# A hybrid decoder step: the sample tokens of the delta-rule group as one masked chunk on TensorE

## The reference, cut to what matters

```python
def step(S, inp):
    rt, wt, kt, vt, kkt, at = inp
    sa = jnp.einsum('nhij,nhj->nhi', S, -kkt)
    S = (S * wt[:, :, None, :] + sa[..., None] * (kkt * at)[:, :, None, :]
         + vt[..., None] * kt[:, :, None, :])
    return S, jnp.einsum('nhij,nhj->nhi', S, rt)
S, y = lax.scan(step, s0.astype(F32), ...)      # over the tokens of a sequence
y = (y - mean(y)) * rsqrt(var(y) + eps)         # per head, then gain, offset, bonus
```

## Time and profile before

| | |
|---|---|
| median of 3 runs | 3367.37 us (3344.56 to 3388.64) |
| the profiled execution's own time | 3341.69 us |
| its span, first to last instruction | 3339.8 us |
| mean granted clock of TensorE | 0.928 of full speed |
| PE busy | 2920.4 us, 87% |
| DVE busy | 1480.7 us, 44% |
| ACT busy | 915.8 us, 27% |
| POOL busy | 83.5 us, 2% |
| the stage `rwkv`, layer 1 | about 1245 to 1452 us of the span |
| the stage `rwkv`, layer 2 | about 2857 to 3066 us of the span |

### The profile page before, as it was taken

The page is one execution under the profiler, slowest core; times in us unless marked ns, Lnnn a source line. Parts: engine busy times, 40 slices in busy tenths (PEclk is TensorE's granted clock), DMA queues, the critical chain, the costliest instruction groups (busy, mean ns, idle before and its releaser), DMA issues. The chain is left out here.

```text
span 3339.8 us, 62897 instructions
## 1 busy us (share of the span) xinstructions
PE 2920.4 (87%) x26036; PEld 2706.7 (81%) x26036; DVE 1480.7 (44%) x2589; ACT 915.8 (27%) x1733; POOL 83.5 (2%) x132
## 2 busy tenths in 40 slices
PE   3999999999887986879889999999988779686995
PEld 2998989997775876769879898899877578675994
DVE  0532253225734567852243225322574347586322
ACT  2322242123221342222142224321322115322222
POOL 0010000000000000000001000000000000000000
PEclk8998999999998998979999999999999869896997
DMA  3322334432233221033223233443323313202431
GB/s 139 91 72 68 84 93 134 136 98 71 51 95 81 64 84 46 3 133 112 85 73 83 62 83 98 112 140 107 85 51 89 93 44 81 72 3 83 127 111 61
DMA packets 413106, 283.74 MB, mean 85 GB/s; under 512 B 44204, under 2 KB 385900, under 8 KB 408334
## 3 DMA queue, kind: packets, MB, share of 16 engines
q1 hardware_dynamic: 412238, 275.19, 29.3%
q10 hardware_dynamic: 576, 4.46, 0.3%
HBM read 243.39 MB, written 36.18 MB: 84 GB/s over the span
## 5 line engine op out<-in xcount | busy, mean ns | idle before, releaser
L359 PE MATMUL acc<-h_hi,in_w_hi 128*128 128x272 f32 x3968 | 904.9, 310 | 40.3 <-SPq L534 18.9
L359 PE MATMUL acc<-h_lo,in_w_hi 128*128 128x272 f32 x3968 | 838.5, 293 | 0.0
L359 PE MATMUL acc<-h_hi,in_w_lo 128*128 128x272 f32 x3968 | 837.5, 293 | 0.0
L359 PEld LDWEIGHTS acc<-h_hi,in_w_hi 128*128 128x128 f32 x3968 | 644.6, 195 | 102.8 <-issue 46.2
L359 PEld LDWEIGHTS acc<-h_lo,in_w_hi 128*128 128x128 f32 x3968 | 642.8, 194 | 0.0
L359 PEld LDWEIGHTS acc<-h_hi,in_w_lo 128*128 128x128 f32 x3968 | 639.4, 194 | 0.0
L386 DVE TENSOR_TENSOR in_w_lo<-in_w_raw,in_w_hi 128x512 fp32r<-128x512 f32 x496 | 349.2, 710 | 482.2 <-ACT in_w_hi L382 479.6
L382 ACT CAST in_w_hi<-in_w_raw 128x512 fp32r<-128x512 f32 x496 | 303.1, 617 | 455.5 <-PE acc L359 373.3
L359 PE MATMUL out_acc<-mix_hi,out_w_hi 128*128 128x272 f32 x1024 | 214.6, 291 | 22.8 <-DVE mix_lo L722 22.7
L359 PE MATMUL out_acc<-mix_hi,out_w_lo 128*128 128x272 f32 x1024 | 213.9, 291 | 0.0
L359 PE MATMUL out_acc<-mix_lo,out_w_hi 128*128 128x272 f32 x1024 | 213.2, 290 | 0.0
(11 more groups left out here) (393 smaller groups left out, 3612.2 us busy)
## 6 DMA issues: line engine op xcount, KB each, us to landing
in_w_raw<-in_w_in SPq DMA_DIRECT2D x488, 256.0 KB, 2.9
region<-in_cache_sb_kv SPq DMA_DIRECT2D x128, 256.0 KB, 3.1
out_w_raw<-in_w_out SPq DMA_DIRECT2D x128, 256.0 KB, 2.7
regions<-in_cache_dsa SPq DMA_DIRECT2D x64, 160.0 KB, 2.1
region<-x_spill SPq DMA_DIRECT2D x8, 1088.0 KB, 9.0
x_spill<-region SPq DMA_DIRECT2D x32, 272.0 KB, 2.1
mix_spill<-mix SPq DMA_DIRECT2D x6, 1088.0 KB, 5.5
mix_back<-mix_spill SPq DMA_DIRECT2D x6, 1088.0 KB, 7.4
```

The source lines that it names most:

```text
L359: last = pe.matmul(self.acc[:, i % 2, c, 0:HALF_N], w[:, u % RING, t, :], part[:, f, HALF_N * c:HALF_N * c + HALF_N], start=first and w is ...
```

## The change

The sample tokens are computed as one chunk of 32 tokens with masks that keep each sequence of 4 to itself (constants `s_before`, `s_upto`, `s_after`, `s_seq`), by the same algebra as the prompt's chunks, in a class `SampleRule`. Its 19 steps are set into segments of iterations 0 to 2 by the table `AT`, on PE, ACT and DVE alike, and `pool` makes three operands on POOL. PSUM grows from four to eight banks; the samples use banks 4 to 7. The state is loaded in eight transfers, one for each head, with 8x64 values for each of 64 partitions, stored in the same way, and transposed on PE both ways (steps 0, 1 and 14, 15). The trips of rows and of y through DRAM, the turning of rows, and the norm at the end are gone. `scan`, `powers` and `scale` of pairs 1 to 3, which stood ahead of iteration 0, now stand in segments 2 to 14 of iteration 0.

```diff
 class DeltaRule:
     def act(self, act):
-        act.activation(k.logw[:, :, NP:NT], k.logw[:, :, NP:NT], ACT.Exp, scale=DECAY).then_inc(kept["decayed"], 1)
-        for n in range(6):
-            act.wait_ge(made["rows"], n + 1)
-            act.copy(self.rows[n], self.bank[0:NS, n % 4, :]).then_inc(kept["rows"], 1)
-            if n < PAIRS:
-                self.powers(act, n)
+        self.powers(act, 0)
+        self.samples.powers(act)
...
+                if it == 0 and seg in (4, 9, 14):
+                    self.powers(act, seg // 5 + 1)
+                self.samples.act(act, it, seg)
...
     def dve(self, dve):
         self.scan(dve, 0)
-        self.scan(dve, 1)
-        for g in range(PAIRS):
-            self.scale(dve, g)
-            if g + 2 < PAIRS:
-                self.scan(dve, g + 2)
+        self.samples.scan(dve)
+        self.scale(dve, 0)
+        self.samples.scale(dve)
...
-                if it == 1 and seg == 2:
-                    dve.wait_ge(self.loaded, 16 * (1 + 2 * NB))
-                    self.samples.choose(dve, step)
-                if 1 <= it <= DS and seg in (3, 8, 13, 16):
-                    if seg == 3:
-                        advance = self.samples.advance(dve, step, self.summed_y, it - 1)
-                    next(advance)
+                if it == 0 and seg in (2, 7, 12):
+                    self.scan(dve, seg // 5 + 1)
+                if it == 0 and seg in (4, 9, 14):
+                    self.scale(dve, seg // 5 + 1)
+                self.samples.dve(dve, it, seg, step)
...
-        dve.wait_ge(kept["back"], 1)
-        center(PAIRS)
-        finish(PAIRS)
     def pool(self, pool):
         unit(0)
+        pool.wait_ge(kept["scaled"], PAIRS)
+        self.samples.pool(pool, self.masked)
     def sp(self, sp):
+        samples.load(sp)
         for g in range(3):
             sp.dma_start(k.mix_back[:, 4 * g:4 * g + 4, :], mix_rows(k)[g]).then_inc(self.mix_came, 16)
...
+class SampleRule:
+    AT = {(0, 0): 0, (0, 1): 1, (0, 2): 2, (0, 3): 3, (0, 5): 4, (0, 6): 5, (0, 8): 6, (0, 10): 7, (0, 11): 8,
+          (1, 2): 9, (1, 3): 10, (1, 5): 11, (1, 8): 12, (1, 11): 13, (1, 14): 14, (1, 17): 15, (2, 2): 16, (2, 4): 17, (2, 13): 18}
+    def load(self, sp):
+        for h in range(H8):
+            r, j = h % 2, h // 2
+            sp.dma_start(self.nat[C * r:C * r + C, j, :, :], self.k.state_wkv[bass.ds(self.l, 1), :, h].rearrange("a s i j -> (a i) s j")).then_inc(self.loaded, 16)
...
+    def pe(self, pe, it, seg):
+        if step in (0, 1):                     # turn the states: 32 matmuls a step
+            if step == 0:
+                pe.wait_ge(self.loaded, 16 * H8)
...
+        elif step == 9:
+            for j, r in each:
+                out = row(bank, r)[:, 7, C * j:C * j + C]
+                last = pe.matmul(out, row(self.ak, r)[:, j, :], row(self.vrow, r)[:, j, :], start=True, stop=False)
+                for s in range(NB):
+                    last = pe.matmul(out, half(self.apart, r)[:, j, NS * s:NS * s + NS], half(self.state, r)[:, j, s, :], start=False, stop=(s == NB - 1))
...
+        elif step == 11:
+            for j, r in each:
+                out = half(bank, r)[:, 5, NS * j:NS * j + NS]
+                pe.matmul(out, row(self.u, r)[:, j, :], row(self.br, r)[:, j, :], start=True, stop=False, skip_group_check=True)
+                pe.matmul(out, row(self.vrow, r)[:, j, :], row(self.ar, r)[:, j, :], start=False, stop=False, skip_group_check=True)
+                for s in range(NB):
+                    last = pe.matmul(out[:, DS * s:DS * s + DS], half(self.state, r)[:, j, s, :], half(self.w, r)[:, j, DS * s:DS * s + DS],
+                                     start=False, stop=(s == NB - 1), skip_group_check=True)
...
+        elif step in (12, 13):
+            for n in range(2):
+                j = 2 * (step - 12) + n
+                for r in range(2):
+                    out = half(bank, r)[:, (6 if step == 12 else 4) + n, :]
+                    pe.matmul(out, row(self.rows, r)[:, 1, j, :], row(self.values, r)[:, j, :, :], start=True, stop=False)
+                    last = pe.matmul(out, row(self.rows, r)[:, 0, j, :], row(self.mine, r)[:, j, :, :], start=False, stop=True)
...
+    def pool(self, pool, masked):
+        pool.memset(self.apart, 0.0).then_inc(kept["cleared"], 1)
+        for t in range(DS):
+            pool.tensor_copy(self.apart[:, :, t:NB * NS:NS + DS], self.kap[:, :, t:NS:DS]).then_inc(kept["spaced"], 1)
+        pool.wait_ge(kept["vrow"], 1)
+        pool.tensor_tensor(self.values, self.vrow[...].to_broadcast([2 * NS, 4, NB, C]), self.c("s_seq")[...], ALU.mult).then_inc(kept["values"], 1)
+        for j in range(4):
+            last = pool.tensor_tensor(self.fresh[:, j, :, :], self.state[:, j, :, :], self.ends[:, j, :].unsqueeze(2).to_broadcast([P, NB, C]), ALU.mult)
```

More of the change, by code:

```diff
@@ L135 @@
 KEPT = AT["chunk_in"][0]
+OWN_D = AT["spread"][0] - KEPT
 SPREAD = AT["spread"][0]
@@ L2174 @@
 ITER, SEGS = PAIRS + 2, 20
-MADE = "rows pair low n2 m2 vrow n4 d2 m4 brow m8 d4 krow dt d q qt q2 z key t x u y total spread final back total_s spread_s".split()
-KEPT_AS = ("rows n rest br m d1 n2 m2 vrow n4 d2 m4 brow m8 d4 krow dt d q qt q2 z ak ar t x u state y "
-           "final back scanned less up down ahead scaled ended decayed gained centered squared logged rooted mixed stepped_o").split()
+MADE = "pair low n2 m2 vrow n4 d2 m4 brow m8 d4 krow dt d q qt q2 z key t x u y total spread final".split()
+KEPT_AS = ("n rest br m d1 n2 m2 vrow n4 d2 m4 brow m8 d4 krow dt d q qt q2 z ak ar t x u state y "
+           "final scanned less up down ahead scaled ended gained centered squared logged rooted mixed normed").split()
+MADE_S = "turned pair low vrow m2 key t rows x u y grown back total spread".split()
+KEPT_S = ("turned n br m d1 vrow m2 ak ar t rows x u y mine values faded grown back spaced cleared "
+          "centered squared logged rooted normed scanned less up down ahead scaled gained aged").split()
 class DeltaRule:
@@ L2200, in __init__ @@
         self.chunk_in = free[:, 3072:3584].rearrange("p (j t) -> p j t", j=4)
-        self.sq = free[:, 3584:4096].rearrange("p (j t) -> p j t", j=4)
+        self.own = free[:, 3072:3072 + OWN_D]
+        self.sq = free[:, 3072 + OWN_D:3584 + OWN_D].rearrange("p (j t) -> p j t", j=4)
         self.ends = sb("dr_ends", [P, NC, 4])
[L2203 to L2208, removed]
         ft = k.ft
-        self.sources = (ft[:, R_SLOT:R_SLOT + 4], k.logw, ft[:, K_SLOT:K_SLOT + 4], ft[:, V_SLOT:V_SLOT + 4], k.kap, k.beta)
+        self.samples = SampleRule(k, l, take, sb, bank, free)
         self.keys, self.values, self.y = ft[:, K_SLOT:K_SLOT + 4], ft[:, V_SLOT:V_SLOT + 4], ft[:, R_SLOT:R_SLOT + 4]
@@ L2242, in pe @@
         eye = k.c("eye64")
[L2243 to L2246, removed]
-            for i in range(4):
-                last = pe.transpose(bank[0:NS, n % 4, P * i:P * i + P], t[:, i, NP:NT], k.c("ident"))
-            last.then_inc(made["rows"], 1)
-        yield 0
         def product(g, name, n, left, right):
```

339 lines of the change are left out of this document (262 added, 77 removed).

## The result

The changed kernel takes 3427.0 us (median of four runs, 3401.3 to 3450.4) against 3359.3 of the kernel before on the same chip: ratio 1.0238, 95% interval 1.0188 to 1.0288. Six more runs gave 1.0183 (1.0100 to 1.0266). Forecast were 3384 us and a range up to 3418, so it is slower than I allowed for. The medians given here are of all runs of a kernel, and a ratio leaves out the runs of either kernel that lie more than 1.5% above its fastest.

The account below looks back on a forecast made before the run. DVE looked like the bound of iterations 1 to 3, but its recurrence mostly hidden behind PE; -10.5 + 11.6 + 17.4 - 0.6 - 2.8 - 6.9 = +8.2 us a layer, +16.4 in all, gave 3384 us, range 3348 to 3418.

Parts of the forecast that it names:

- 3, *Iteration 1, +17.4 us: Iteration 1 of each layer: recurrence goes, the samples' matmuls come on PE; 56.0 us for 38.6, +17.4.
- x 4.2 to 8.4, y 4.0 to 8.0: Samples' x and y matmuls on PE in iteration 1: 58.5 to 117 ns each; taken 6.3 and 6.0 us.
- Steps 12 and 13: Samples' 16 matmuls of 512 columns on PE in iteration 1: 7.5 to 15 us, low end 7.5 taken.
- rival (c): Changes of matmul form at the samples' steps each cost 0.19 us: +10.6 us a layer, 3405 us; chance 0.09.
- Head -10.5: Stage's head: pair waits only for scan, powers and scale of pair 0, so starts 10.5 us sooner.
- Iteration 0 +11.6: Iteration 0: later pairs' scans and scales on DVE, samples' transposes and small steps on PE; 40.6 us for 29.0.
- Iteration 2: Without the recurrence t and the totals start sooner, but the samples' two totals on PE take 2.0 us: -0.6 us.
- Iteration 3: Without the recurrence t starts 1.9 us sooner and the totals 1.0, with 0.3 coming back: -2.8 us.
- Iteration 4 and the end: Iteration 4: 0, nobody waits for its recurrence; end: -6.9 us, no wait for `sample_y`, the prompt's last norm ends it.
- (b): Halves don't overlap in runs, in steps 9 to 15 of iteration 1: +23.2 us a layer, 3414 us; chance 0.12.
- (a): Matmuls overlap and fill gaps, long runs at the low end: -3.9 us a layer, 3360 us; chance 0.22.
- (d): Gain is what DVE's share promised, iterations 1 to 3 fall to PE's work: -18.5 us a layer, 3330; chance 0.05.

Follow-up runs that it names:

- e1: The changed kernel with the halves r alternating from matmul to matmul in the samples' x and y (steps 9 and 11): 3373.8 us, ratio 1.0037.
- b1: The kernel before, without the recurrence's arithmetic on VectorE (trips to DRAM, waits and stores stay): 3325.9 us, ratio 0.9924.

## Why the prediction was wrong

The step that failed is 3, *Iteration 1, +17.4 us*, and in it two terms: "x 4.2 to 8.4, y 4.0 to 8.0 ... I take the middle for the long runs". The rest of the step held. Without the samples I had iteration 1 at 27.1 + 4.8 = 31.9 us; the kernel without the recurrence has 32.6. Steps 12 and 13 are 7.3 us (taken 7.5), the transposes 3.7 (3.8), and u is 1.0 at the low clock and 0.6 in e1 (0.5).

x and y failed by order and by clock. The order: at the full clock a group of x takes 1.23 us and a group of y 1.37, that is 9.8 and 11.0 us, above even my high ends of 8.4 and 8.0, since a matmul in a run of one half takes 128 ns (two records of 64) and two interleaved halves do two in the same time. My bound of 117 ns was twice the right row; I took the middle because runs of two go at full speed, and from two in a row nothing follows for nine. The rule that I quoted from the Trainium skill ("TensorE: Matmul & The Clock Gate", part 3, "The mechanism": a weight load overlaps matmuls in flight only in another row group) fits the trace of after, 64 ns a record against 32; but the halves here differ in the partitions that they write as well, and no run tells the two apart, nor why runs of two go free. The changes of form cost little, as I said against rival (c): two records with another form ahead of 16 take 0.23 us, 0.1 more than two in the row, for two changes.

The clock: no term and no rival had a fall of it, only the last sentence ("a PE clock below 1.00 in iteration 1"). It is 8 of the 28.8 us, and some 3.3 more in the prompt's products behind both runs (e1 gains 20.3 from key to key, 17.0 of it in x and y).

With this one term mended, the sum comes out right, in part by luck. e1 has x and y at 5.0 and 6.8 us, close to the 6.3 and 6.0 in my sum, and its stages are 7.4 and 7.6 us longer than before; the forecast was 8.2 a layer. It measures 1.0037, and the forecast was 1.005. Up to the last key product e1 is 19.6 us longer than before, where the sum has 15.1, and from there on 12.1 shorter, where it has 6.9: two errors of some 5 us that cancel.

The other steps. Head -10.5: it is -10.6 (8.5 us for 19.1). Iteration 0 +11.6: +13.9, with brow at 17.4 us from pair, dt at 24.7 and q2 at 34.3 (walked: 17.9, 25.0, 34.5); the missing 2.3 us are the products behind q2, whose first rows are on the slow clock after the longest wait:

```profile
1279.35 1.15 PE L2254 MATMUL dr_bank<-region 64*64 64x64 f32 x32 [3.57 <-DVE region L2576]
1281.17 1.97 PE L2254 MATMUL dr_bank<-dr_d,scratch 64*64 64x64 f32 x32 [0.68 <-ACT scratch L2436]
...
1288.04 1.20 PE L2274 MATMUL dr_bank<-regions 64*64 64x128 f32 x18 [0.18 <-DVE dr_ar L2550]
```

Iteration 2: 38.0, as forecast. Iteration 3: -2.6 from key to key (forecast -2.8). Iteration 4 and the end together, from the last key product: 36.9 us for 49.0, where I had -6.9; the difference of 5.2 us is most likely the recurrence of the last token, which I counted at nothing in iteration 4 (b1, without it but with the trip through DRAM, is 7.3 us shorter from there to the end). The state's load and POOL made no one wait. So the layers are 27.7 and 24.5 us longer, and 20 of each is what x and y took beyond my 12.3, the slowed products behind them included.

Of the rivals, (b) named the right mechanism and gave it 0.12 and 3414 us; it was off in taking steps 12 and 13 into it (their runs of two overlap) and in having no clock. That its 23.2 us a layer is near the measured 27.7 and 24.5 is these two errors offsetting each other. (a) and (d) are out by iteration 1.

## What to carry to other kernels

Where matmuls use one half of the partitions, write the loop so that the halves alternate innermost; here a run of nine or ten in one half cost twice its time and the clock fell in it, while runs of two cost nothing. When a price has a row only for short runs, take the end that the mechanism gives for long ones as the forecast, and the cheap end as the rival (here even that end, 16.4 us for x and y, was 4.4 short of the 20.8 at the full clock). Work moved from a side engine to the bound engine has to be paid in its gaps: in iteration 1, which had no room, the samples' 23.4 us of e1 cost 25.3 (57.9 for 32.6 without them); moved to the end, 11 of 25.7 us were gained.

## What was not expected of the hardware

TensorE's granted clock fell to its lower level (0.50) while the engine was busy without a gap: in the profile of after 4.6 us into matmuls in one half and 5.2 us into 4-column ones, and in x it did not fall once the halves alternated (1.00 through 5.0 us). In code that no version touched (128x128 weights; 256 of 597 records with 4 columns, the others with 128 or 272) it stayed at 0.50 for 129.7 us in five of fourteen profiles, and at 0.99 in others of the same program, with PE busy 127 to 130 us of 130 either way; 60 us hang on it. What starts such a spell stays open.
